# Decode attention: TensorE's steps taken in pairs

## The chip, the cores and the metric

The kernel runs on one core of one Trainium2 chip (trn2). The metric is the device time of one execution in microseconds (us). All inputs and outputs lie in the chip's memory (HBM).

## The reference, cut to what matters

One layer of a decoder: a mixer and an FFN, for a prompt of 256 tokens and for 8 samples of 8 new tokens each. The change touches the attention of the samples over their caches. Each sample b has 8 "fox" heads over 2048 cached keys (16 pages of 128, found by a page table, with a bias per key) and 12 "dilated" heads in three groups over cached windows of 128, 512 and 2048 keys.

```python
def fox_attend(q, k, v, bias_q, bias_k, q_pos, k_pos):
    s = jnp.einsum('bqhd,bshd->bhqs', q, k) * ATTN_SCALE + bias_q + bias_k      # cut
    p = jax.nn.softmax(jnp.where(causal, s, NEG_INF), axis=-1)
    return jnp.einsum('bhqs,bshd->bqhd', p, v)
def dilated_group_attend(q, k_all, v_all, q_idx, window, dil, table_g):
    kg, vg = k_all[:, idx_c], v_all[:, idx_c]                                    # every dil-th key
    s = jnp.einsum('bqhd,bqnhd->bhqn', q, kg) * ATTN_SCALE + rel
    lse = jax.nn.logsumexp(s, axis=-1)
    return jnp.einsum('bhqn,bqnhd->bqhd', jnp.exp(s - lse[..., None]), vg), lse
def merge_out(h, o_fox, o_dil, w_gate, b_gate, w_o_fox, w_o_dil, w_out):
    gates = jax.nn.sigmoid(jnp.einsum('bsd,de->bse', h, w_gate) + b_gate)
    g_fox, g_dil = jnp.split(gates, 2, axis=-1)
    return jnp.einsum('bse,ed->bsd', g_fox * y_fox + g_dil * y_dil, w_out)
```

The gates do not depend on the attention; the kernel computes most of them beside it.

## The kernel before

Everything is written out by hand, per engine, with semaphores; no scheduler moves anything. Each engine runs its own function `sequence(q, kb, vb)`. It is called as sequence 0 (keys of sample 0, no values), then seven times with the keys of sample kb = b and the values of sample vb = b-1, then once with the values of sample 7 alone. A sequence has 24 steps (STEPS), n = 0 to 23. Cached keys and values of a sample come in 23 blocks (KPG) each: 16 pages, one block of the first window, two of the second, four of the third. A block is 512 KB, the first window's 256 KB.

A step n of TensorE before the change:

- `transposes(kb, n)`: the keys of block n are turned, four 128x128 pieces into PSUM bank 2 (L1042) and four into bank 3 (L1047). ScalarE copies bank 2 to SBUF (L1428, semaphore ke_a), VectorE bank 3 (L1872, ke_b). Each bank has one buffer, so the next transposes wait for these copies.
- `gate_part(q, n)`: a share of the gate projection. A unit is 128 output channels, in 16 parts (128 input channels each) of three matmuls (L1031 to L1033, 320 columns). GATE_UNITS gives the units per sequence (2, 3, 3, 3, 4, 3, 3, 3, 1), spread evenly: with three units each step of a sequence has two parts, six matmuls.
- `fox_scores(kb, n // 2 - 1)` in even steps from 2 to 16: scores of two key blocks, eight matmuls into four column tiles of the array, 32 columns wide (L1067). VectorE adds the bias from PSUM to SBUF and takes the maximum (`fox_out`, L1877).
- `dil_scores` in steps 17 to 23 (L1081), column tiles too. `turn_fox` in steps 19 to 22: transposes of the fox probabilities (L1097), which ScalarE copies (`fox_probs`). The exponential that they need is ScalarE's `fox_exp`, in its steps 17 and 18, L1437.
- `values(vb, n)`: values of block n with the probabilities of sample vb, four matmuls for a page, in column tiles (L1127, L1133). `fox_new_values` (L1142) and `dil_new_values` (L1152) add the new tokens.
- `turn_dil` (L1104), `turn_out` (L1161), and `turn_dil_new` (L1111), which waits for ScalarE's copy of what `turn_dil` wrote.

The splits: gate weights come as fp32 panels and are split into a high part (ScalarE, L1395) and a low part (VectorE, L1837), in two halves per unit. The unit behind the next one is split 4 steps (for an even unit) or 1 step (for an odd one) after a unit is done, and its second half a step later (`splits_due`). In VectorE's program a step is: `keys_b(n)`, in even steps `fox_out`, then what `gates_after` has due. In ScalarE's it is `keys_a(n)`, then the softmax's part, then `gates_after`.

GpSimd issues the loads in the order key block n, value block n. kraw has 3 buffers, vraw 4: a load of block n waits until block n-3 is transposed, or block n-4 of the values is used. At step 1 it issues four bias loads for the sample (L705). SP issues the gate weights.

Of the kernel before, what the change touches and what calls it, by code (L numbers as in the profile page):

```python
# [40 lines left out]
NPG = PAST // PAGE  # L41
# [6 lines left out]
KPG = NPG + 1 + 2 + 4  # L48
# [95 lines left out]
def build(nc, I, O, scratch):  # L144
    with ExitStack() as ctx:
# [198 lines left out]
        STEPS = KPG + 1  # L344
# [462 lines left out]
        def _(pe):  # L807
# [13 lines left out]
            for n in range(12):  # L821
                t, q = divmod(n, 4)
# [202 lines left out]
            def gate_part(q, n):  # L1025
                for u, k in gate_work(q, n):
                    if k == 0:
                        pe.wait_ge(lo_done, u + 1)
                        pe.wait_ge(acc_free, u + 1)
                    acc = ps[:, u % 2, 0:T]  # L1030
                    pe.matmul(acc, w_hi[:, u % 2, k, :], act_hi[:, k, :], start=(k == 0), stop=False)  # L1031
                    pe.matmul(acc, w_hi[:, u % 2, k, :], act_lo[:, k, :], start=False, stop=False)  # L1032
                    mm = pe.matmul(acc, w_lo[:, u % 2, k, :], act_hi[:, k, :], start=False, stop=(k == KT - 1))  # L1033
                    if k == KT - 1:
                        mm.then_inc(unit_done, 1)

            def transposes(b, s):
                n = b * KPG + s
                pe.wait_ge(k_ld[n % KRING], loads_before(b, s, KRING))
                wait_pos(pe, ke_a, n)  # L1040
                for j in range(4):
                    mm = pe.transpose(ps[:, 2, P * j:P * j + P], kraw[:, n % KRING, P * j:P * j + P], ident[:])  # L1042
                mm.then_inc(tr_a, 1)
                if s != NPG:
                    wait_pos(pe, ke_b, narrow(b, s))
                    for j in range(4):
                        mm = pe.transpose(ps[:, 3, P * j:P * j + P], kraw[:, n % KRING, P * (4 + j):P * (5 + j)], ident[:])  # L1047
                    mm.then_inc(tr_b, 1)
# [22 lines left out]
            def dil_scores(b, s):  # L1071

                pe.wait_ge(ke_a, b * KPG + s + 1)
                if s != NPG:
                    pe.wait_ge(ke_b, narrow(b, s) + 1)
                else:
                    pe.wait_ge(qd_ok, b + 1)
                    wait_pos(pe, pd_ev, 2 * b)
                for r, g, c, n in residues(s):
                    for h in range(HG):  # L1080
                        mm = pe.matmul(ps[32 * h:32 * h + DT, 5, P * g:P * g + P], qd[:, 32 * n + DT * h:32 * n + DT * h + DT],  # L1081
                                       kT[:, s // 2 % 2, HG * r + h, P * (s % 2):P * (s % 2) + P], start=(n == 0), stop=False, **mmx)
                if s == KPG - 1:
                    for g in range(NG):
                        for h in range(HG):
                            mm = pe.matmul(ps[32 * h:32 * h + DT, 5, NG * P + DT * g:NG * P + DT * g + DT],
                                           sT[:, HF + HG * g + h, DT * b:DT * b + DT],
                                           sT[:, NQ + HF + HG * g + h, DT * b:DT * b + DT], start=False, stop=(g == NG - 1), **mmx)
                mm.then_inc(sc_done, 1)
# [17 lines left out]
            def turn_dil_new(b):  # L1107

                pe.wait_ge(pd_ev, 2 * b + 1)
                for g in range(NG):  # L1110
                    mm = pe.transpose(ps[0:DT, 5, P * g:P * g + P], ds_[:, NG * P + DT * g:NG * P + DT * g + DT], ident[:])  # L1111
                mm.then_inc(pd_tr, 1)
# [53 lines left out]

            def sequence(q, kb, vb):

                for n in range(STEPS):
                    if kb is not None and n < KPG:  # L1170
                        transposes(kb, n)
                    gate_part(q, n)
                    if vb is not None and n == 2:
                        turn_dil(vb)
                        if vb > 0:
                            turn_out(vb - 1)
                    if vb is not None and n == 3:
                        turn_dil_new(vb)
                    if kb is not None:
                        if n == 2:  # L1180
                            pe.wait_ge(zero_ps, 1)
                            fox_new_scores(kb)
                        if 2 <= n <= NPG and n % 2 == 0:
                            fox_scores(kb, n // 2 - 1)
                        if n > NPG:
                            dil_scores(kb, n - 1)
                        if 19 <= n < 23:
                            turn_fox(kb, n - 19)
                    if vb is not None and n < KPG:
                        values(vb, n)  # L1190
                        if n == NPG:
                            fox_new_values(vb)
                        if n == KPG - 1:
                            dil_new_values(vb)

            sequence(0, 0, None)
            for b in range(1, DB):
# [970 lines left out]
```

## Time and profile before

| | us |
|---|---|
| median of 3 runs | 2484.23 |
| lowest, highest | 2477.99, 2488.96 |
| the profiled execution | 2484.29 |
| its span, first to last instruction | 2482.7 |
| TensorE matmul busy | 2348.4 |
| VectorE busy | 1065.7 |
| ScalarE busy | 812.7 |
| decode attention, from the first key transposes to the last values | about 578 to 1280 |

In the profile PE is TensorE, PEld its weight loads, DVE VectorE, ACT ScalarE, POOL GpSimd, SP the engine that only issues transfers. Busy matmul times overlap, since matmuls are pipelined; how long something takes on TensorE is read from start to start. Each fp32 matmul is recorded as two, so eight score matmuls stand as x16. "[0.50 <-DVE kT L1872]" behind a row is idle time in front of it and who ended it.

### The profile page before, as it was taken

What the parts mean: (1) busy time and instruction counts of PE and PEld (TensorE: products, weight loads), DVE (VectorE), ACT (ScalarE), POOL (GpSimd) and SP (SyncE); (2) the same over time, 40 slices, a digit from 0 to 9 for tenths busy, and PEclk for the clock granted to TensorE, in tenths of its full rate; (3) what the DMA queues carried; (4) which work ended last, traced back from release to release, by engine and by line L of the source; (5) the groups of instructions that cost most, each with busy time, mean ns of one, the idle gap of its engine ahead of it and who ended that gap; (6) DMA issues with size and microseconds to landing.
All of it is one profiled execution on the core that took longest, in us unless ns stands there. A gap on an engine that the chain in (4) does not pass through costs nothing.

```text
span 2482.7 us, 45242 instructions
## 1 busy us (share of the span) xinstructions
PE 2348.4 (95%) x18252; PEld 2140.8 (86%) x18252; DVE 1065.7 (43%) x1433; ACT 812.7 (33%) x982; POOL 468.8 (19%) x877
## 2 busy tenths in 40 slices
PE   7999999997889999999989996999999999999997
PEld 6999999996666666666659995999999999999997
DVE  6443443433333333333326436444444444444445
ACT  3233333332333333333312334333333332333334
POOL 2110000101333333333311232111111111111221
PEclk8999999998999999999989997999999999999998
DMA  8554343545899999999976654676676766688883
GB/s 251 158 168 148 113 148 128 183 132 169 288 339 346 342 313 346 351 339 309 339 255 208 193 160 135 228 238 238 227 248 219 250 230 235 226 282 267 286 301 101
DMA packets 340126, 585.85 MB, mean 236 GB/s; under 512 B 20624, under 2 KB 283092, under 8 KB 336304
## 3 DMA queue, kind: packets, MB, share of 16 engines
q0 software_dynamic: 70752, 309.02, 35.2%
q1 hardware_dynamic: 269232, 274.86, 34.8%
q8 instruction: 99, 1.62, 0.3%
q14 instruction: 43, 0.34, 0.0%
HBM read 564.06 MB, written 109.39 MB: 271 GB/s over the span
## 4 chain that ended last, share of the span: by engine, by line
PE 79%; DMA 11%; issue 4%; DVE 3%; ACT 2%; POOL 1%; POOLq 0%; SPq 0%; DVEq 0%; ACTq 0%
PE ps L815 14%; PE ps L817 14%; PE ps L816 14%; DMA kraw<-in_cache_fox_k 6%; PE ps L853 6%; PE ps L855 6%; PE ps L854 6%; PE ps L1042 3%; PE ps L1047 2%; DMA kraw<-in_cache_win_k 2%; PE ps L1067 2%; PE ps L1127 1%; PE ps L1031 1%; PE ps L1033 1%; PE ps L1032 1%
## 5 line engine op out<-in xcount | busy, mean ns | idle before, releaser
L1626 DVE TENSOR_TENSOR w_lo<-raw,w_hi 128x2048 fp32r<-128x2048 f32 (+2 forms) x250 | 525.5, 2102 | 791.7 <-ACT w_hi L1295 785.4
L1295 ACT ACTIVATE w_hi<-raw 128x2048 fp32r<-128x2048 f32 (+2 forms) x250 | 439.2, 1757 | 1054.0 <-PE ps L817 741.5
L815 PE MATMUL ps<-act_hi,w_hi 128*128 128x320 f32 x1616 | 500.7, 310 | 5.7 <-DVE gs L2059 5.7
L817 PE MATMUL ps<-act_hi,w_lo 128*128 128x320 f32 x1616 | 500.5, 310 | 0.0
L816 PE MATMUL ps<-act_lo,w_hi 128*128 128x320 f32 x1616 | 500.5, 310 | 0.0
L853 PE MATMUL ps<-act_hi,w_hi 128*128 128x320 f32 x1040 | 327.6, 315 | 0.0
L855 PE MATMUL ps<-act_hi,w_lo 128*128 128x320 f32 x1040 | 321.4, 309 | 0.0
L854 PE MATMUL ps<-act_lo,w_hi 128*128 128x320 f32 x1040 | 321.3, 309 | 0.0
L815 PEld LDWEIGHTS ps<-act_hi,w_hi 128*128 128x128 f32 x1616 | 304.4, 188 | 5.9 <-issue 5.9
L816 PEld LDWEIGHTS ps<-act_lo,w_hi 128*128 128x128 f32 x1616 | 304.4, 188 | 0.0
L817 PEld LDWEIGHTS ps<-act_hi,w_lo 128*128 128x128 f32 x1616 | 304.3, 188 | 0.0
L1872 DVE COPY kT<-ps 128x512 f32<-128x512 f32 x176 | 121.4, 690 | 232.0 <-PE ps L1047 231.5
L1428 ACT ACTIVATE kT<-ps 128x512 f32<-128x512 f32 x184 | 109.7, 596 | 314.3 <-PE ps L1042 314.1
L853 PEld LDWEIGHTS ps<-act_hi,w_hi 128*128 128x128 f32 x1040 | 195.5, 188 | 0.8 <-issue 0.5
L854 PEld LDWEIGHTS ps<-act_lo,w_hi 128*128 128x128 f32 x1040 | 195.5, 188 | 0.1
L855 PEld LDWEIGHTS ps<-act_hi,w_lo 128*128 128x128 f32 x1040 | 195.2, 188 | 0.0
L1042 PEld LDWEIGHTS ps<-ident,kraw 128*128 128x128 f32 x736 | 80.6, 144 | 108.3 <-issue 49.9
L785 POOL TENSOR_TENSOR tick<-tick 1x1 f32<-1x1 f32 x144 | 28.5, 198 | 718.1 <-PE ps L817 708.0
L1042 PE MATMUL ps<-ident,kraw 128*128 128x128 f32 x736 | 124.3, 293 | 33.3 <-DMA kraw<-in_cache_fox_k 28.4
L1031 PE MATMUL ps<-act_hi,w_hi 128*128 128x320 f32 x400 | 145.0, 362 | 2.0 <-DVE w_lo L1626 2.0
L1033 PE MATMUL ps<-act_hi,w_lo 128*128 128x320 f32 x400 | 126.4, 316 | 0.0
L1032 PE MATMUL ps<-act_lo,w_hi 128*128 128x320 f32 x400 | 126.3, 316 | 0.0
(374 smaller groups left out, 3753.6 us busy)
## 6 DMA issues: line engine op xcount, KB each, us to landing
raw<-in_w_gate_up SPq DMA_DIRECT2D x88, 1024.0 KB, 6.3
kraw<-in_cache_fox_k POOLq DMA_DIRECT2D x128, 512.0 KB, 6.9
vraw<-in_cache_fox_v POOLq DMA_DIRECT2D x128, 512.0 KB, 7.5
raw<-in_w_in SPq DMA_DIRECT2D x60, 1024.0 KB, 7.6
raw<-in_w_gate SPq DMA_DIRECT2D x32, 1024.0 KB, 15.3
raw<-in_w_down SPq DMA_DIRECT2D x32, 1024.0 KB, 6.1
out_win_k_sample<-in_cache_win_k POOLq DMA_DIRECT2D x64, 510.0 KB, 5.8
out_win_v_sample<-in_cache_win_v POOLq DMA_DIRECT2D x64, 510.0 KB, 4.2
```

What stands on the lines that cost most here:

```text
L815: pe.matmul(ps[:, bk_, 0:T], w_hi[:, slot, k, :], xh[:, x_k, :], start=(k == k0), stop=False)
L816: pe.matmul(ps[:, bk_, 0:T], w_hi[:, slot, k, :], xl[:, x_k, :], start=False, stop=False)
L817: mm = pe.matmul(ps[:, bk_, 0:T], w_lo[:, slot, k, :], xh[:, x_k, :], start=False, stop=(k == k1 - 1))
L853: pe.matmul(acc, w_hi[:, u % 2, k, :], act_hi[:, k, :], start=(k == 0), stop=False)
L854: pe.matmul(acc, w_hi[:, u % 2, k, :], act_lo[:, k, :], start=False, stop=False)
L855: mm = pe.matmul(acc, w_lo[:, u % 2, k, :], act_hi[:, k, :], start=False, stop=(k == KT - 1))
L1031: pe.matmul(acc, w_hi[:, u % 2, k, :], act_hi[:, k, :], start=(k == 0), stop=False)
L1032: pe.matmul(acc, w_hi[:, u % 2, k, :], act_lo[:, k, :], start=False, stop=False)
L1033: mm = pe.matmul(acc, w_lo[:, u % 2, k, :], act_hi[:, k, :], start=False, stop=(k == KT - 1))
L1042: mm = pe.transpose(ps[:, 2, P * j:P * j + P], kraw[:, n % KRING, P * j:P * j + P], ident[:])
L1295: act.activation(w_hi[:, slot, 0:kt, :], raw[:, pslot, 0:kt, P * slot:P * slot + P], ACT.Copy).then_inc(hi_done, 1)
L1626: dve.tensor_tensor(w_lo[:, slot, 0:kt, :], raw[:, pslot, 0:kt, P * half:P * half + P], w_hi[:, slot, 0:kt, :].bitcast(F32), ALU.subtract) ...
```

## The change

Only TensorE's `sequence` changes. It takes two steps at a time. The gate matmuls of both stand between the two key transposes; behind the second come the fox scores, and both steps' dilated scores and values in one stretch. The transposes of the probabilities move beside the key transposes: parts 0 and 2 behind the transposes of steps 19 and 21, part 1 behind those of step 20, part 3 in front of the last stretch. `turn_dil_new` moves from step 3 to step 2. What TensorE computes, and the programs of the other engines, stay.

```diff
--- before.py
+++ after.py
@@ -1166,32 +1166,40 @@
 
             def sequence(q, kb, vb):
 
-                for n in range(STEPS):
-                    if kb is not None and n < KPG:
+                for n in range(0, STEPS, 2):
+                    if kb is not None:
                         transposes(kb, n)
+                        if n == 20:
+                            turn_fox(kb, 1)
                     gate_part(q, n)
+                    gate_part(q, n + 1)
                     if vb is not None and n == 2:
                         turn_dil(vb)
                         if vb > 0:
                             turn_out(vb - 1)
-                    if vb is not None and n == 3:
-                        turn_dil_new(vb)
                     if kb is not None:
+                        if n == 22:
+                            turn_fox(kb, 3)
+                        elif n + 1 < KPG:
+                            transposes(kb, n + 1)
+                        if n in (18, 20):
+                            turn_fox(kb, n - 18)
                         if n == 2:
                             pe.wait_ge(zero_ps, 1)
                             fox_new_scores(kb)
-                        if 2 <= n <= NPG and n % 2 == 0:
+                        if 2 <= n <= NPG:
                             fox_scores(kb, n // 2 - 1)
-                        if n > NPG:
-                            dil_scores(kb, n - 1)
-                        if 19 <= n < 23:
-                            turn_fox(kb, n - 19)
-                    if vb is not None and n < KPG:
-                        values(vb, n)
-                        if n == NPG:
-                            fox_new_values(vb)
-                        if n == KPG - 1:
-                            dil_new_values(vb)
+                    if vb is not None and n == 2:
+                        turn_dil_new(vb)
+                    for m in (n, n + 1):
+                        if kb is not None and m > NPG:
+                            dil_scores(kb, m - 1)
+                        if vb is not None and m < KPG:
+                            values(vb, m)
+                            if m == NPG:
+                                fox_new_values(vb)
+                            if m == KPG - 1:
+                                dil_new_values(vb)
 
             sequence(0, 0, None)
             for b in range(1, DB):
```

TensorE in a pair of fox steps of sequence 1, before (gates, fox scores, values, key transposes, gates):

```order
L1031 MATMUL ps<-act_hi,w_hi 128x320
L1032 MATMUL ps<-act_lo,w_hi 128x320
L1033 MATMUL ps<-act_hi,w_lo 128x320
L1067 MATMUL ps<-kT,qf 16x256 x8
L1127 MATMUL ps<-vraw,pt 16x256 x4
L1042 MATMUL ps<-ident,kraw 128x128 x4
L1047 MATMUL ps<-ident,kraw 128x128 x4
L1031 MATMUL ps<-act_hi,w_hi 128x320
```

and after (gates, key transposes, fox scores, values of both blocks, next transposes, gates):

```order
L1031 MATMUL ps<-act_hi,w_hi 128x320
L1032 MATMUL ps<-act_lo,w_hi 128x320
L1033 MATMUL ps<-act_hi,w_lo 128x320
L1042 MATMUL ps<-ident,kraw 128x128 x4
L1047 MATMUL ps<-ident,kraw 128x128 x4
L1067 MATMUL ps<-kT,qf 16x256 x8
L1127 MATMUL ps<-vraw,pt 16x256 x8
L1042 MATMUL ps<-ident,kraw 128x128 x4
L1047 MATMUL ps<-ident,kraw 128x128 x4
L1031 MATMUL ps<-act_hi,w_hi 128x320
```

The second key transposes now stand in front of the scores, and the next key transposes follow right behind the values.

TensorE at the probabilities' transposes (L1097), before, behind the gates of a step:

```order
L1033 MATMUL ps<-act_hi,w_lo 128x320
L1081 MATMUL ps<-kT,qd 8x128 x8
L1097 MATMUL ps<-ident,fs 128x128 x4
L1133 MATMUL ps<-vraw,pg 16x256 x4
L1042 MATMUL ps<-ident,kraw 128x128 x4
L1047 MATMUL ps<-ident,kraw 128x128 x4
L1031 MATMUL ps<-act_hi,w_hi 128x320
L1032 MATMUL ps<-act_lo,w_hi 128x320
```

and after, the same part and its neighbours:

```order
L1042 MATMUL ps<-ident,kraw 128x128 x4
L1047 MATMUL ps<-ident,kraw 128x128 x4
L1097 MATMUL ps<-ident,fs 128x128 x4
L1081 MATMUL ps<-kT,qd 8x128 x8
L1133 MATMUL ps<-vraw,pg 16x256 x4
L1081 MATMUL ps<-kT,qd 8x128 x8
L1133 MATMUL ps<-vraw,pg 16x256 x4
```

Between tiles before, now directly behind the key transposes.

VectorE, step 12 and 13 of sequence 1; its line numbers are 8 higher after the change, its order is the same (key copy of step 12, bias add, low part of the weight split, key copies of steps 13 and 14):

```order
L1880 COPY kT<-ps 128x4x128
L1885 ISA fs,fm<-ps,fb 128x256
L1885 ISA fm 128x1
L1845 TENSOR_TENSOR w_lo<-raw,w_hi 128x1024
L1880 COPY kT<-ps 128x4x128 x2
```

The copy of step 13 stands behind the bias add and the split, though the transposes that it copies are now issued before the scores that the bias add waits for.

## Rows read from the trace of the kernel before

**Rows 1.** Waits of TensorE from 700 to 1250 us: us in total, times, longest us.

```profile
PE ps L1042 <- DMA kraw<-in_cache_fox_k: 17.0, 20, 1.9
PE ps L1127 <- DMA vraw<-in_cache_fox_v: 16.8, 8, 4.5
...
PE ps L1047 <- DVE kT L1872: 1.5, 3, 0.5
```

**Rows 2.** Busy time by stretch: stretch, its length, each engine's busy us, PEclk, DMA share, GB/s.

```profile
578.00:660.00 82.00, 62.66 (x615) 49.35 (x613) 33.45 (x70) 29.99 (x46) 22.41 (x39) 0.86 0.73 212
660.00:1235.00 575.00, 529.96 (x5784) 382.75 (x5781) 195.85 (x427) 198.44 (x346) 188.92 (x354) 0.97 0.96 339
1235.00:1290.00 55.00, 44.48 (x338) 25.05 (x332) 12.67 (x22) 13.34 (x23) 14.01 (x25) 0.84 0.81 268
```

**Rows 3.** TensorE in order of time, one pair of steps: start us, us, what, count.

```profile
1009.25 1.06 PE L1067 MATMUL ps<-kT,qf 128*16 128x256 f32 x16
1010.12 0.61 PE L1127 MATMUL ps<-vraw,pt 128*16 128x256 f32 x8
1010.66 0.66 PE L1042 MATMUL ps<-ident,kraw 128*128 128x128 f32 x4
1011.16 0.60 PE L1047 MATMUL ps<-ident,kraw 128*128 128x128 f32 x4
1011.51 0.39 PE L1031 MATMUL ps<-act_hi,w_hi 128*128 128x320 f32 x1
...
1012.32 0.31 PE L1033 MATMUL ps<-act_hi,w_lo 128*128 128x320 f32 x1
1012.56 0.62 PE L1127 MATMUL ps<-vraw,pt 128*16 128x256 f32 x8
1013.12 0.66 PE L1042 MATMUL ps<-ident,kraw 128*128 128x128 f32 x4
```

**Rows 4.** TensorE in order of time in sequence 0: gate matmuls, then key transposes.

```profile
608.81 0.31 PE L1033 MATMUL ps<-act_hi,w_lo 128*128 128x320 f32 x1
608.96 0.60 PE L1042 MATMUL ps<-ident,kraw 128*128 128x128 f32 x4
609.40 0.60 PE L1047 MATMUL ps<-ident,kraw 128*128 128x128 f32 x4
```

**Rows 5.** TensorE in order of time, two steps with dilated scores.

```profile
714.79 0.62 PE L1081 MATMUL ps<-kT,qd 128*8 128x128 f32 x16
715.23 0.62 PE L1133 MATMUL ps<-vraw,pg 128*16 128x256 f32 x8
...
716.93 0.66 PE L1047 MATMUL ps<-ident,kraw 128*128 128x128 f32 x4 [0.50 <-DVE kT L1872]
...
718.40 0.62 PE L1081 MATMUL ps<-kT,qd 128*8 128x128 f32 x16
718.95 0.66 PE L1097 MATMUL ps<-ident,fs 128*128 128x128 f32 x4
719.54 0.63 PE L1133 MATMUL ps<-vraw,pg 128*16 128x256 f32 x8
```

**Rows 6.** VectorE in order of time: bias add, weight split, key copy; and the copy at 716.

```profile
716.20 0.68 DVE L1872 COPY kT<-ps 128x512 f32<-128x512 f32 x1
...
1010.37 0.42 DVE L1877 CUSTOM_DVE_ANT_0 fs<-ps,fb 128x256 f32<-128x256 f32 x1 [0.42 <-PE ps L1067]
...
1010.72 1.22 DVE L1837 TENSOR_TENSOR w_lo<-raw,w_hi 128x1024 fp32r<-128x1024 f32 x1
1011.86 0.68 DVE L1872 COPY kT<-ps 128x512 f32<-128x512 f32 x1
```

**Rows 7.** ScalarE in order of time: table load and first exponential of the softmax.

```profile
1048.74 1.28 ACT L1437 ACT_TABLE_LOAD   x1
1050.03 1.15 ACT L1437 ACTIVATE fs<-fs,fm 128x1024 f32<-128x1024 f32 x1
```

**Rows 8.** DMA issues by line: count, KB each, median us to landing.

```profile
kraw<-in_cache_fox_k POOLq DMA_DIRECT2D x128, 512.0 KB, 6.9
```

## The prediction

> **What bounds the kernel now.** I read four views: the waits of TensorE, the busy time by stretch, the order of time on TensorE over a few steps, and the order of time on the engines that empty PSUM for it. The change touches only the stretch of decode attention: 184 key blocks (23 for each of 8 samples b), one step each, and a 24th step per sample that has gates alone. The stretch has three parts [rows 2]. In the first (keys of sample 0, no values; sequence 0) TensorE is busy 62.66 of 82 us. In the long middle (seven sequences with keys of b and values of b-1) it is busy 529.96 of 575 us. In the tail (values only) it is busy 44.48 of 55 us, with the loads as its pace. In the middle the DMA engines are busy 0.96 of the time too, so two resources are nearly full together. TensorE waited for key blocks 20 times, 17.0 us, and for value blocks 8 times, 16.8 us with a longest of 4.5 us [rows 1]. Those long ones stand at the head of each sequence, where the bias rows are loaded. The rest of the middle runs at TensorE's pace, so an instruction gap on TensorE is time of the kernel there, as long as nothing takes its place.
>
> One pair of steps before, by starts [rows 3] (T = eight key transposes, G = six gate matmuls, S = fox scores, V = values of one block): S to V 0.87 us, V to T 0.54 to 0.56, inside T 0.50, then 0.35 to the first G, G to V 1.05. The pair T G V T G S V is 0.85 + 1.05 + 0.56 + 0.85 + 1.05 + 0.87 + 0.54 = 5.77 us.
>
> **The change part by part.** The pair becomes T G G T S V V.
> - Pitch inside G: 0.145 us (last gate to the transposes behind it, 0.15 [rows 4], so going from gates to transposes costs nothing). The first gate behind transposes has 0.23 us: 1012.32 minus 1011.51 is 0.81, less four pitches. Two G in one are 0.23 + 11 x 0.145 = 1.83 us.
> - Transposes behind gates: 0.44 for the first four [rows 4] instead of 0.50. The four before tiles take 0.59 between tile matmuls on both sides (L1097) [rows 5], less 0.06 for the entry: 0.53. The second T is 0.97 us.
> - V before another V, without the way back to the full array: eight S matmuls take 0.87, so four take 0.43 instead of 0.55.
> - Sum: 0.85 + 1.83 + 0.97 + 0.87 + 0.43 + 0.55 = 5.50 us, 0.27 to 0.28 less. With 12 pairs in 7 sequences: 84 x 0.28 = 23.5 us.
> - The four transposes of the probabilities (L1097) per sample stood between tile matmuls: dilated scores to V is 0.44 directly and 0.55 + 0.59 with them [rows 5], 0.70 more. Beside other transposes they cost 0.44. That is 0.26 less, 28 times in the middle, 7.3 us, and 1.0 us in sequence 0.
> - In sequence 0 there are no values. Two steps had T G T G S; T G G T S has the same sum, since the saved entries are paid back at the transposes in front of the tiles. Nothing there but the 1.0 us.
> - In the tail the loads set the pace (268 GB/s, TensorE idle 10 of 55 us [rows 2]). I take 0; at most 12 x 0.2 us.
> - The small transposes L1111 go from step 3 to step 2, behind S. What they wait for (ScalarE's copy of the first four) has the second T and S, 1.8 us, as its cover. I take 0; 0.5 us a sequence if the cover fails.
>
> Gain on TensorE alone: 31.8 us.
>
> What it adds is on VectorE, whose own order stays. It copies the second half of the keys of step n, adds the bias to S (L1877), does a weight split if one is due in step n, and then copies the keys of step n+1. Before, the transposes of n+1 came after S, so this queue had a whole step. Now they stand before S, and the next transposes into the same bank come after S V V. Counted from the start of S, those want the bank at 0.87 + 0.43 + 0.55 + 0.50 = 2.35 us. VectorE starts the bias add 1.12 us after S (1009.25 to 1010.37) [rows 3, 6], its next instruction 0.35 later, and a copy takes 0.69. TensorE goes on 0.05 us after a copy ends (716.20 + 0.68 against 716.93 [rows 5, 6]). Free at 2.21 us: a pair without a split just passes, with 0.14 us to spare.
> - With a split behind the bias add (next start 1.14 us later [rows 6]) the bank is free at 3.34 us: TensorE waits 1.0 us, and all behind it. By the rule that sets the splits one falls on an even step from 4 to 12 in 11 cases of the middle (12; 4, 8; 12; 4, 6; 4, 8; 12; 4, 8 in sequences 1 to 7): 11 us.
> - On step 16 there are four (sequences 1, 3, 4, 6), with more tile work in front: 0.6 us each, 2.4 us.
> - The softmax. ScalarE begins it when the maximum is there, behind S of step 16, which now stands after the transposes of 17. Table 1.28 and exponential 1.15 us [rows 7], then where one is due a weight split, and only then the next keys. I get 0.4 us more than now in three sequences and 1.2 in sequence 4: 2.4 us.
> - Sequence 0 has no V as cover. The bank is wanted at 0.87 + 0.12 + 0.50 = 1.49 us and free at 2.21: 0.7 us in each of 7 pairs, 1.8 in that of step 16, 6.8 us. About 2 us of small key waits in that stretch vanish in them: 4.7 us.
>
> Cost: 11 + 2.4 + 2.4 + 4.7 = 20.5 us. Bounds of this block: 0 (if something of these waits is always there already) and 41, twice, if later key loads follow each late bank.
>
> The loads. GpSimd asks for key block n when block n-3 has been transposed. Before, the lead was three steps less a T, 3 x 2.89 - 0.85 = 7.8 us. Now it is 7.35 us for both blocks of a pair (3.65 us into a pair to the start of the next but one, 11.0). A block lands in 6.9 us [rows 8]. With the DMA engines at 0.96 nothing is gained where they are full: at the head of each sequence and while a panel of gate weights comes in, some 3 to 4 of 12 pairs. I take 5 us given back; bounds 0 and all of the net gain, 11.
>
> Sum: -31.8 + 20.5 + 5 = -6 us. The profiled execution took 2484.29 us, at the median of 2484.23: 2478 us.
>
> **The rivals.**
> - The gain comes whole: the bank waits fall where TensorE would wait for blocks anyhow, or VectorE gets to the copy sooner. For it: the splits come near panel loads, where waits for keys stand now. Against it: the loads keep 0.96. Without the bank waits -31.8, less some 7 us more of block waits, as 0.96 cannot go much over 1 (0.04 x 575 = 23 us is all that is left in the middle): -25, 2459 us.
> - The loads are the bound: what TensorE saves, it waits for blocks, and of the bank waits sequence 0's remain. For it: rows 2. Against it: between the heads the pair has run at 5.77 us. 0 to +3 us, 2485 us.
> - Slower: emptying PSUM decides in every pair, the place being the transposes behind S V V. The spare there is 0.14 us. If VectorE comes that much later, or V V is shorter, all 41 pairs without a split wait as well; with 0.5 us each, the size of the wait seen now for this bank [rows 5], it is 20 us more: 2498 us. It decides from 0.14 us on. For it: the spare is a difference of pipelined starts. Against it: each start was read at full clock. The Trainium skill, "TensorEngine Tiling (Array Packing)", section "PSUM Bottleneck", says that with tiles TensorE speeds up but the emptying of PSUM does not and may become the limit; by that rule this case is the outcome, and the trace so far shows the bank's copy as the releaser of L1047 three times, 1.5 us in all [rows 1].
> - That the change does nothing: two mode changes a pair go, and I have read their price from starts, so this has almost no chance.
>
> **How the numbers follow.** Likeliest case (2478, own range 2468 to 2487) 0.50; gain whole 0.22; loads the bound 0.15; slower by every pair 0.13. Less than 0.5%, 12.4 us, cannot be told from no change. The first case passes that bound downward about one time in seven, the second nearly always, the fourth about two times in three upward. Faster 0.28, same 0.62, slower 0.10. For 8 in 10 the range reaches from the second case to just short of the fourth: 2458 to 2494 us.
>
> **What would show it.** The pair from T to T without a split 5.50 us, with one 6.5. TensorE's waits before L1047 released by VectorE's key copy, 1.5 us before [rows 1], near 15 to 20 us in all, the longest 1.0 us, and seven of 0.7 in sequence 0. The probability transposes 0.44 us behind T. Waits for kraw and vraw in sum a few us above 34. I am wrong if the L1047 waits stay under 5 us, if they appear in pairs without a split in the middle, or if the waits for blocks grow by over 15 us.

## The result: no faster, and slower by 7 us

| | median of 20 runs, us | lowest, highest |
|---|---|---|
| before | 2480.49 | 2473.82, 2493.98 |
| after | 2487.47 | 2477.86, 2499.22 |

The ratio is 1.0028, with a 95% interval of 1.0015 to 1.0041: 7 us more (3.7 to 10.2). That is inside the range and inside 0.5%, but the sign of the forecast, 6 us less, was wrong. The profiled execution of after took 2493.41 us (span 2491.8), at the upper end of its runs; a second one, r1_after, took about 2480. Of before there is a second one too, r0_before (span 2479.8). Single profiles of one kernel differ by up to 13 us, so below I use both where a sum over a stretch is taken.

What TensorE waited for in the profile after, 700 to 1250 us, in the columns of [rows 1]:

```profile
PE ps L1127 <- DMA vraw<-in_cache_fox_v: 24.8, 6, 6.0
PE ps L1042 <- DMA kraw<-in_cache_fox_k: 19.6, 22, 2.6
PE ps L1047 <- DVE kT L1880: 9.9, 15, 0.8
...
PE ps L1111 <- ACT pn L1461: 2.4, 1, 2.4
```

The wait for VectorE's copy of the key bank rose from 1.5 us in 3 places [rows 1] to 9.9 us in 15 (in the second profiles from 2.5 us in 5 to 9.9 in 15). The wait for value blocks rose from 16.8 to 24.8 us, and its longest from 4.5 to 6.0. The second profile of either kernel says the same, r0_before first, then r1_after:

```profile
PE ps L1127 <- DMA vraw<-in_cache_fox_v: 18.0, 7, 4.6
PE ps L1042 <- DMA kraw<-in_cache_fox_k: 13.2, 18, 1.5
```

```profile
PE ps L1127 <- DMA vraw<-in_cache_fox_v: 29.6, 8, 6.6
PE ps L1042 <- DMA kraw<-in_cache_fox_k: 16.9, 18, 2.7
```

The same three stretches as in [rows 2], after:

```profile
578.00:660.00 82.00, 62.16 (x607) 49.95 (x605) 30.00 (x65) 29.13 (x46) 21.80 (x38) 0.88 0.69 195
660.00:1235.00 575.00, 509.68 (x5725) 394.55 (x5729) 193.93 (x432) 200.62 (x347) 188.25 (x354) 0.96 0.97 340
1235.00:1290.00 55.00, 40.35 (x341) 20.58 (x330) 10.09 (x19) 10.90 (x20) 11.65 (x22) 0.74 0.72 237
```

In the middle TensorE is busy 20 us less of 575 than in [rows 2], for 1% fewer records (5725 against 5784); in the second profiles it is 15 us less for 30 records more. The DMA share is 0.97 where it was 0.96, and 340 GB/s where it was 339. So TensorE got its work done in less time, and most of that time turned into waits.

A pair of steps on TensorE in the profile after, then a pair with a split in it, in the columns of [rows 3]:

```profile
767.47 0.66 PE L1042 MATMUL ps<-ident,kraw 128*128 128x128 f32 x4
...
770.17 0.60 PE L1042 MATMUL ps<-ident,kraw 128*128 128x128 f32 x4
770.60 0.60 PE L1047 MATMUL ps<-ident,kraw 128*128 128x128 f32 x4
771.13 1.06 PE L1067 MATMUL ps<-kT,qf 128*16 128x256 f32 x16
772.00 1.05 PE L1127 MATMUL ps<-vraw,pt 128*16 128x256 f32 x16
772.98 0.66 PE L1042 MATMUL ps<-ident,kraw 128*128 128x128 f32 x4
774.48 0.65 PE L1047 MATMUL ps<-ident,kraw 128*128 128x128 f32 x4 [0.84 <-DVE kT L1880]
...
779.55 0.66 PE L1042 MATMUL ps<-ident,kraw 128*128 128x128 f32 x4
```

From transposes to transposes the first takes 772.98 - 767.47 = 5.51 us (forecast 5.50), the second 779.55 - 772.98 = 6.57 (forecast 6.5). VectorE in the second, in order of time:

```profile
772.25 0.42 DVE L1885 CUSTOM_DVE_ANT_0 fs<-ps,fb 128x256 f32<-128x256 f32 x1 [2.96 <-PE ps L1067]
...
772.61 1.22 DVE L1845 TENSOR_TENSOR w_lo<-raw,w_hi 128x1024 fp32r<-128x1024 f32 x1
773.74 0.68 DVE L1880 COPY kT<-ps 128x512 f32<-128x512 f32 x1
```

The bank had been full since 771.2, and VectorE stood idle 2.96 us in front of the bias add, since its order puts the scores first. Then came the split, and only then the copy, which ends at 774.42. TensorE goes on at 774.48: 1.50 us from the first four transposes to the second, where it is 0.50 without the wait, so the price is the 1.0 us of the forecast (the view counts 0.84 of it as idle). In order of time the 15 waits are eleven of 0.84 and four of 0.16; the four stand at step 16. These are the 11 and 4 splits that the forecast counted.

The transposes of the probabilities, after, behind those of the keys:

```profile
723.46 0.60 PE L1047 MATMUL ps<-ident,kraw 128*128 128x128 f32 x4
723.90 0.60 PE L1097 MATMUL ps<-ident,fs 128*128 128x128 f32 x4
724.25 0.39 PE L1031 MATMUL ps<-act_hi,w_hi 128*128 128x320 f32 x1
```

They start 0.44 us behind those of the keys, and the gates follow 0.35 us later.

Waits of TensorE in sequence 0 (578 to 660 us), after:

```profile
PE ps L1042 <- DMA kraw<-in_cache_fox_k: 8.6, 2, 8.4
PE ps L1047 <- DVE kT L1880: 6.4, 7, 3.3
```

Of the 6.4 us, 3.3 is one wait that before has as well (3.3 us, once, in the same view of before). The other six are the new ones, 0.5 us each as idle time. In order of time, a pair of sequence 0:

```profile
610.24 1.06 PE L1067 MATMUL ps<-kT,qf 128*16 128x256 f32 x16
611.23 0.66 PE L1042 MATMUL ps<-ident,kraw 128*128 128x128 f32 x4
612.46 0.66 PE L1047 MATMUL ps<-ident,kraw 128*128 128x128 f32 x4 [0.57 <-DVE kT L1880]
```

From start to start it is 1.23 us instead of 0.50: 0.73, the forecast's 0.7.

Sequence 0 has one more cost, which is not in the forecast. In before, the first fox scores run at 592.58, and then TensorE waits for the load of step 3 until 600.94. In pairs these scores stand behind the transposes of step 3, so they come after that wait and no longer in front of it:

```profile
600.46 1.12 PE L1042 MATMUL ps<-ident,kraw 128*128 128x128 f32 x4 [8.41 <-DMA kraw<-in_cache_fox_k]
603.10 1.91 PE L1067 MATMUL ps<-kT,qf 128*16 128x256 f32 x16 [0.42 <-DVE fm L1885]
604.94 1.12 PE L1042 MATMUL ps<-ident,kraw 128*128 128x128 f32 x4
```

From the transposes of step 3 to those of step 4 it is 604.94 - 600.46 = 4.48 us, the same in r1_after, against 2.57 and 2.56 in the two traces of before: 1.9 us. From step 4 to step 16, where five of the six new bank waits lie, it is 30.4 and 29.2 against 27.7 and 27.5.

To see where the time goes I read the start of single instructions in each trace and divided the stretch in three: sequence 0 from the first key transpose to the first `turn_dil`; six sequences from there to the seventh `turn_dil`; the last from there to the last `dil_new_values`.

| us | sequence 0 | six of the middle | last |
|---|---|---|---|
| before, r0_before | 85.0, 82.2 | 500.6, 503.8 | 112.9, 114.0 |
| after, r1_after | 89.1, 89.0 | 502.0, 495.1 | 113.7, 111.9 |
| mean difference | +5.4 | -3.7 | -0.6 |

The middle of one kernel differs by 7 us between its two profiles. Two kernels below, e2 and e3, have the middle of after unchanged: 498.1 and 498.6 us, so -3.7 holds.

These sum to +1; the two profiled pairs differ by +4 in their spans, and the 20 runs by +7. So 3 us of the profiled difference lie outside the attention of the samples, where the program is the same, and some 3 us more are in the runs but not in these profiles. I could not place those.

### The profile page after: what moved, and what is told of

Same layout as the page of the kernel before. It is cut to its first block, busy times and chain, and to the rows that moved or that the text cites. A ratio compares the mean times of both kernels' runs of the same rounds, so it can differ in the third digit from the quotient of the medians.

```text
span 2491.8 us, 45242 instructions
## 1 busy us (share of the span) xinstructions
PE 2333.2 (94%) x18252; PEld 2159.0 (87%) x18252; DVE 1060.5 (43%) x1433; ACT 813.7 (33%) x982; POOL 468.2 (19%) x877
## 4 chain that ended last, share of the span: by engine, by line
PE 79%; DMA 10%; DVE 4%; issue 4%; POOL 1%; ACT 1%; POOLq 0%; SPq 0%; DVEq 0%; ACTq 0%
PE ps L815 14%; PE ps L816 14%; PE ps L817 14%; DMA kraw<-in_cache_fox_k 6%; PE ps L853 6%; PE ps L855 6%; PE ps L854 6%; PE ps L1047 3%; PE ps L1042 2%; PE ps L1067 2%; PE ps L1031 2%; PE ps L1032 1%; PE ps L1033 1%; PE ps L1127 1%; DMA raw<-in_w_gate 1%
## 5 line engine op out<-in xcount | busy, mean ns | idle before, releaser
L785 POOL TENSOR_TENSOR tick<-tick 1x1 f32<-1x1 f32 x144 | 29.2, 203 | 716.4 <-PE ps L817 706.2
```

## The experiments

Each kernel was timed against before in the same batch; the ratios are to before.

**Both kernels again.** No edit.

> The kernel before once more, for a second profile. In the first one TensorE waited 37.6 us for key and value blocks in the middle and stood at the slow clock level for 34 us of it; five profiles of kernels with the paired middle show 44 to 49 us and 41 to 48 us. If pairs are the cause, this one lies under those again (35 to 40 us and 30 to 38 us). If the first profile was chance, it lies among them.

> The changed kernel once more, as the mark for the three beside it. Both theories expect what was seen, a ratio to before of 1.0015 to 1.0041. The trace shows how far one profile stands for the next: waits of TensorE for VectorE's key copy near 6 us in sequence 0 and 10 us in the middle; the waits for value blocks at the heads of the sequences, and those of the tail, may differ by some us from the first profile.

Measured: 2480.29 us, 0.9994 [0.9982, 1.0006], and 2486.4 us, 1.0027 [1.0014, 1.0040]. The difference stands.

**The copy ahead of the bias add.** After, with VectorE's copy of odd steps 3 to 17 in front of the scores' bias add:

```diff
-                        if n < KPG and n != NPG:
+                        if n < KPG and n != NPG and not (n % 2 and 2 < n <= NPG + 1):
                             keys_b(kb, n)
+                        if n % 2 == 0 and 2 <= n <= NPG:
+                            keys_b(kb, n + 1)
```

> VectorE takes the key copy of each odd step from 3 to 17 in front of the bias add of the even step before it. Theory 1 (the waits for the bank cost the change its gain): the waits before L1047 in sequence 0 and the middle fall from 16 us to under 3, and the time falls by 12 to 16 us against the changed kernel, to about 10 us under the kernel before. Theory 2 (the loads take back what TensorE saves): the same waits fall, sequence 0 gets its 4 to 5 us back, but in the middle the waits for key and value blocks grow by as much as the bank waits fall, and the time falls by 4 to 6 us, to that of the kernel before.

Measured: 2478.03 us, 0.9995 [0.9984, 1.0007], 8.4 us less than after (give or take 4), between what the two theories expected. TensorE's waits of this kernel, 700 to 1250 us:

```profile
PE ps L1127 <- DMA vraw<-in_cache_fox_v: 29.8, 9, 7.1
PE ps L1042 <- DMA kraw<-in_cache_fox_k: 20.0, 24, 2.9
PE ps L1067 <- DVE fm L1885: 4.4, 6, 0.7
```

The 9.9 us of bank waits are gone (0.6 is left, once), for 1.9 us more in front of the scores (4.4 against 2.5). VectorE now copies before it adds, and the bank is free when the next transposes come:

```profile
771.04 0.69 DVE L1880 COPY kT<-ps 128x512 f32<-128x512 f32 x1 [1.93 <-PE ps L1047]
772.06 0.42 DVE L1885 CUSTOM_DVE_ANT_0 fs<-ps,fb 128x256 f32<-128x256 f32 x1 [0.33 <-PE ps L1067]
```

So the bank waits cost time, though they stand beside waits for blocks: with light loads (l_e1, below) the same edit brings 9.6 us, about as much. Without them the paired kernel only equals before; most of the 31.8 us saved on TensorE is still not there. In sequence 0 the edit shortens the stretch from step 4 to step 16 to 27.3 us, as short as before. The 1.9 us in front of it stay (from step 3 to step 4 it is 4.76), and the whole sequence takes 88.9 us in this one profile, as long as in after, since it waits some 1 us longer each for a load at its start (9.55 against 8.41) and for the value block at its end (4.7 against 3.5).

**One end of the stretch step by step.** TensorE's old loop for the last sequence alone, and for sequence 0 alone:

```diff
-            sequence(DB, None, DB - 1)
+            single_sequence(DB, None, DB - 1)
```

```diff
-            sequence(0, 0, None)
+            single_sequence(0, 0, None)
```

> Only the last sequence (values of sample 7 alone) is taken step by step as before. If pairs cost the tail its 4 us by bunching the releases of the value buffers, the stretch from the last key scores to the last values falls by 3 to 4 us and so does the time. If the 4 us were chance of one profile, stretch and time stay within 1 us.

Measured: 2484.38 us, 1.0013 [1.0000, 1.0025]: 2 us less than after, which these runs can't tell from nothing.

> Only sequence 0 (keys of sample 0 alone) is taken step by step as before. Theory 1 and the prediction's own term: sequence 0 is 4 to 5 us shorter than in the changed kernel (from the first to the second bias load 61 to 62 us instead of 66) and the time falls by as much. Rival: the loads behind set when the middle starts, and the time stays within 1 us.

Measured: 2479.65 us, 1.0008 [0.9994, 1.0022]: 7 us less than after. Its sequence 0 takes 85.9 us, against 89.1 and 89.0, and from step 3 to step 4 it is 2.57 us again. By time and by trace pairing costs 3 to 7 us in sequence 0.

**Lighter loads.** These leave work out, as their expectations say. For samples 1 to 7 `l` halves the value loads and drops the bias loads; in `x` key and value blocks bring a quarter, and the bias loads are dropped too. The edit of `l`, without VectorE's wait for the dropped loads:

```diff
-                pool.dma_start(vraw[:, n % VRING, 0:src.shape[1]], src)
+                w = src.shape[1] if n < KPG else src.shape[1] // 2
+                pool.dma_start(vraw[:, n % VRING, 0:w], src[:, 0:w])
...
-                        if n == 1:
+                        if n == 1 and kb == 0:
                             load_bias(kb)
```

> The order of before with the loads relieved: value blocks of samples 1 to 7 bring half of their columns (the rest is what stood in the buffer), and the bias rows of sample 0 serve all samples. It is the mark for the next one. Both theories: DMA share in the middle near 0.75, no long waits for value blocks, 25 to 45 us faster than before.

> The changed order with the same relief (half of the value columns, bias of sample 0 alone). Theory 2 (the loads take back what TensorE saves): with room in the loads the gain on TensorE shows, and this is 8 to 14 us faster than the relieved kernel of before (31.8 less 20.5 of my sum). Theory 1, that the bank waits or something else on the chip's engines cost as much as is gained: it is within 3 us of it or slower.

> The relieved loads (half of the value columns of samples 1 to 7, bias of sample 0 alone) with the changed order and the key copy of the odd step in front of the bias add. Theory 2 expects that here, where the loads have room, the bank waits are worth their length: 8 to 13 us faster than the relieved changed kernel, 2410 to 2415 us. Theory 1 expects the same here and the same 8 to 13 us at full loads, where 8.4 us were measured with both sequence 0 and the middle mended.

> The order of before with the loads taken far below their limit: key and value blocks of samples 1 to 7 bring a quarter of their columns, and the bias rows of sample 0 serve all (the rest of each block is what stood in the buffer). A mark for the next two: DMA share in the middle near 0.4, waits for blocks in the middle under 3 us, a pair of steps at 5.77 us.

> The changed order with the same quarter loads. If my sum for TensorE and VectorE was right (31.8 us gained, 20.5 paid), 9 to 13 us faster than its mark. If the gain was sized too high, 5 to 8 us as with half of the values left out.

> The same quarter loads with pairs in the middle alone and the key copy of the odd step in front of the bias add. If the sum was right, 25 to 30 us faster than its mark (30.8 gained, 2.4 paid for the softmax). If the gain was sized too high, 15 to 20 us.

Measured (c1 is paired in the middle alone, with the copy first; see below):

| loads | before | after | with the copy first |
|---|---|---|---|
| full | 2480.5 | 2487.5 | e1 2478.0, c1 2474.3 |
| l | 2430.7, 0.9802 [0.9774, 0.983] | 2423.2, 0.9766 [0.974, 0.9792] | l_e1 2413.5, 0.9719 [0.9697, 0.974] |
| x | 2416.9, 0.9753 [0.9729, 0.9776] | 2413.1, 0.9729 [0.9708, 0.9749] | x_c1 2397.7, 0.9656 [0.9634, 0.9679] |

l_before was to be 25 to 45 us under before, at a DMA share of 0.75; it is 49, at 0.86. The same edit of TensorE's order gives +7 with full loads and -7.5 with `l` (8 to 14 were expected). With `x` it gives -3.8, under both expectations (9 to 13 and 5 to 8), and x_c1 is 19.2 us faster than x_before, in the lower one (15 to 20) and not in the one that goes with my sum (25 to 30). The traces say where the rest of the sum went. In `x` the middle no longer waits for blocks. Busy time of x_before and then x_after, 660 to 1150 us, columns of [rows 2]:

```profile
660.00:1150.00 490.00, 480.47 (x5365) 347.69 (x5366) 185.93 (x408) 184.82 (x324) 168.29 (x313) 1.00 0.47 149
```

```profile
660.00:1150.00 490.00, 471.48 (x5501) 369.67 (x5505) 185.53 (x422) 190.97 (x332) 173.50 (x322) 1.00 0.48 153
```

and the largest waits of x_after from 660 to 1165 us (line numbers are 2 higher; L1049 is L1047):

```profile
PE ps L1049 <- DVE kT L1882: 11.9, 18, 0.8
PE ps L1044 <- ACT kT L1438: 3.2, 5, 1.2
...
PE ps L1044 <- DMA kraw<-in_cache_fox_k: 0.8, 1, 0.8
```

Here pairing saves what TensorE's sum says. The six middle sequences go from 455.6 to 441.6 us, 14.0 less; by my terms without the loads they would be (23.5 + 7.3 - 11 - 2.4 - 2.4) x 6/7 = 12.9 less. With the copy first they take 433.8, 21.8 less, where all but the softmax's 2.4 us would give 24.3. The ends lose: sequence 0 2.4 us (80.7 to 83.1), the last one 4.5 (98.8 to 103.3), so by the traces 7.1 are left, by the times 3.8. The last one loses in its tail: from the last but one `dil_new_values` to the last takes 40.6 us against 34.8 (x_c1, with the old order there, 33.1). The values of two steps now stand together, so their buffers come free together and the next loads are asked for together; that is my reading of it, and no run tests it. TensorE waits there for values, in x_after, 1150 to 1240 us:

```profile
PE ps L1129 <- DMA vraw<-in_cache_fox_v: 7.1, 4, 3.6
```

In x_before it is 2.7 us. With full loads the tail's pace is another, and it shows no such loss: 45.3 and 47.2 us before, 48.2 and 45.2 after.

**The bias loads.** At step 1 of each sequence GpSimd issues four loads (L705), which read 8 rows, each 8 times over. GpSimd and TensorE there, before:

```profile
726.07 2.27 POOL L705 DMA_DIRECT2D fb<-scratch_fb  x4
```

```profile
742.27 0.62 PE L1127 MATMUL ps<-vraw,pt 128*16 128x256 f32 x8 [4.08 <-DMA vraw<-in_cache_fox_v]
```

and after:

```profile
728.42 2.26 POOL L705 DMA_DIRECT2D fb<-scratch_fb  x4
```

```profile
744.80 1.05 PE L1127 MATMUL ps<-vraw,pt 128*16 128x256 f32 x8 [5.31 <-DMA vraw<-in_cache_fox_v]
```

From the issue of the bias loads to TensorE's use of the value block behind them it is 16.20 us before and 16.38 after. Over seven sequences, by the same reading, TensorE came to that block 11.8 us behind the issue in both traces of before, and waited 2.9 and 2.7 us. In the two of after it came 11.1 and 10.9 us behind, and waited 4.05 and 4.0. In one of the seven the block had landed before TensorE came, in both traces of before; over the other six, from issue to block, it is 15.1 and 14.9 us before, 15.6 and 15.4 after. So TensorE comes 0.8 us earlier and the block does not, rather later; why later is not shown.

Why TensorE comes earlier is in the order. The bias loads are issued when block 21's keys have been transposed. In pairs these transposes stand behind both gate parts, so 0.9 us of gate work moved from behind the issue to in front of it. But the dilated scores and values of step 20, 0.9 us too, moved the other way, from in front of these transposes to behind them. The two cancel. What is left is the gain itself: in a full sequence TensorE had seven separate stretches of column-tile work from the issue up to that block, and now has three.

From that block to the next issue it took 68.4 and 68.6 us, now 67.9 and 67.15: 1.0 less, where the light loads show 2.3 less for a whole sequence. So at this one place 0.8 us a sequence is saved and waited away, and with the later block the wait is 1.3 us longer, 9 us over seven sequences. Two pairs of kernels bear on it. In `f` the bias loads of samples 1 to 7 are left out (and VectorE's wait for them):

```diff
-                        if n == 1:
+                        if n == 1 and kb == 0:
                             load_bias(kb)
```

> The order of before with full value loads, but the bias rows of sample 0 serve all samples (seven of eight groups of four bias loads left out). If these loads make the long wait at the head of each sequence, the waits for value blocks in step 1 (some 20 us in the middle) go, and it is 25 to 40 us faster than before.

> The changed order with the bias loads of samples 1 to 7 left out. If what is given back goes at the heads of the sequences (behind the bias loads), this is 5 to 10 us faster than the same kernel in the order of before. If it goes all along the middle, because the key and value loads have no room, the two are within 3 us.

> The kernel before with the bias loads of samples 1 to 7 left out, once more and with more rounds: 2441 to 2445 us, six sequences of the middle in 470 to 475 us.

> The changed kernel with the same loads left out, with more rounds. If the heads take the gain back: the middle keeps its 9 to 11 us over six sequences, sequence 0 costs 4, and it is 3 to 8 us faster than the same kernel in the order of before. If the key and value loads take it all along: within 2 us, and the middle shorter by less than 5 us.

Measured: f_before 2442.13, 0.9843 [0.9818, 0.9868], and again 2443.27, 0.9851 [0.9829, 0.9873]; f_after 2442.96, 0.9856 [0.9826, 0.9886], and again 2441.85, 0.9853 [0.9829, 0.9877]. The means of nine runs each are 2443.5 and 2443.6, give or take 3. Without bias loads pairing costs nothing where it cost 7 us with them, so the heads account for about 7 us by the times, near the 9 that I read there. It gains nothing either, though. The profiles of `f` show the middle 8 us shorter (472.6 and 466.7 to 463.0 and 460.3; with all loads it was 3.7) and sequence 0 3.5 longer, which would be 4.5 less; the times don't show it. So neither expectation of f2_after came whole: the times fit the second, the middle the first. Who holds the rest shows beside `l`: it differs from `f` in one thing, that half of each value block is loaded, and there pairing gains 7.5 us and makes the middle 9.8 us shorter. In `x`, with a quarter of each key and value block, the middle is 14.0 us shorter. So the loads of the blocks themselves hold the rest.

In `p` the bias is written 8 times to memory ahead, so that 64 different rows are read. Nothing is left out:

```diff
-        fbd = nc.dram_tensor("scratch_fb", (DB, HF, NPG * P), F32, kind="Internal").ap()
+        fbd = nc.dram_tensor("scratch_fb", (DB, HF, DT, NPG * P), F32, kind="Internal").ap()
...
-                    rows = fbd[b, 2 * j:2 * j + 2].unsqueeze(1).broadcast_to([2, DT, PAST])
-                    pool.dma_start(fb[32 * j:32 * j + 2 * DT, :], rows)
+                    pool.dma_start(fb[32 * j:32 * j + 2 * DT, :], fbd[b, 2 * j:2 * j + 2].rearrange("h q n -> (h q) n"))
```

> The kernel before with the bias written eight times to memory ahead of the decode stretch (64 stores of 64 KB instead of 8), so that the four loads of each sample read 64 different rows instead of the same 8 rows eight times. If it is the repeated reading of the same rows that slows all packets (4 KB packets took 159 ns as a rule and about 400 ns beside these loads), the waits at the heads go and it is 20 to 35 us faster than before. If it is the writing of 64 rows of 8 KB each into one partition, nothing changes, and it is the same or slower by the stores.

Measured: 2466.2 us, 0.9943 [0.9923, 0.9962], 14 less. I had looked for 20 to 35. From issue to block it is 13.65 us there, with a wait of 1.5 (over the six heads with a wait). How the bias is read is a part of what these loads cost, not all. That it is the reading of the same rows is not shown: the edit also turns each load's source from 2 rows repeated 8 times into 16 rows in one dimension, and reading a row again does not make a packet slow by itself: the 8 KB packets from 660 to 1235 us, nearly all of them of these loads, have a median of 652 ns in before and 920 in p_before.

**The best of both.** Pairs in the seven middle sequences, the old loop at both ends, the copy first in the middle; then the same with the bias of `p`:

```diff
-            sequence(0, 0, None)
+            single_sequence(0, 0, None)
...
-            sequence(DB, None, DB - 1)
+            single_sequence(DB, None, DB - 1)
...
-                        if n < KPG and n != NPG:
+                        if n < KPG and n != NPG and not (q and n % 2 and 2 < n <= NPG + 1):
                             keys_b(kb, n)
+                        if q and n % 2 == 0 and 2 <= n <= NPG:
+                            keys_b(kb, n + 1)
```

> Pairs in the seven middle sequences alone, sequence 0 and the last one step by step as before, and in the middle the key copy of the odd step in front of the bias add. It leaves out all of my sum's costs but the softmax (2.4 us), and keeps 30.8 us of gain on TensorE. Theory 1 (bank waits and sequence 0 are what made the change slower): 15 to 25 us faster than before. Theory 2 (the loads have no room): 0 to 6 us faster than before, with bank waits under 2 us in the middle and 45 to 55 us of waits for blocks.

> All data loaded: pairs in the middle alone, key copy of the odd step in front of the bias add, and the bias written eight times so that no row is read twice. If the two add up it is 21 to 25 us faster than before (7.7 and 14.2 us, and some of the waits for blocks less): 2455 to 2461 us. If the loads stay the bound all along the middle, the bias stores bring their 14 us and the pairs 3 us at most: 2463 to 2467 us.

Measured: c1_best 2474.32 us, 0.9969 [0.9958, 0.998], 6 to 8 less than before, just above what the second theory expected (0 to 6) and far from the first (15 to 25). p_c1 2463.35 us, 0.993 [0.9911, 0.9948], the fastest with all the work in it, as its second expectation had it; beside p_before the pairs bring 3 us, less than the runs can tell. Both are faster than before and after, by less than 1%. In c1 TensorE still waits this much from 700 to 1250 us:

```profile
PE ps L1127 <- DMA vraw<-in_cache_fox_v: 30.1, 9, 6.6
PE ps L1042 <- DMA kraw<-in_cache_fox_k: 17.2, 25, 1.6
```

47 us for blocks, where [rows 1] has 34 and r0_before 31. Of some 25 us that these pairs save over seven sequences where no block is waited for (x_c1, 21.8 in six), 13 to 16 stand here as waits.

The granted clock moved too. From 660 to 1235 us, p_before and then p_c1:

```profile
660.00:1235.00 575.00, 533.07 (x5877) 379.87 (x5875) 202.64 (x438) 205.81 (x360) 192.12 (x366) 0.99 0.98 348
```

```profile
660.00:1235.00 575.00, 523.59 (x5876) 402.61 (x5876) 203.42 (x439) 208.35 (x361) 192.07 (x364) 0.96 0.98 348
```

These means stand for 12 and 46 us at the lower level (1.2 GHz). For before and after they are 0.97 and 0.96, 32 and 44 us; for r0_before and r1_after 34 and 44. The stretches at the lower level follow waits, in after mostly those at the heads, as at the value block that is waited for until 744.80:

```profile
736.20:739.60 3.40, 3.29 (x29) 2.60 (x28) 2.11 (x7) 3.35 (x7) 1.06 (x2) 1.00 1.12 176
739.60:743.00 3.40, 0.00 (x0) 0.00 (x0) 0.35 (x4) 0.44 (x1) 1.05 (x2) 0.87 1.04 164
743.00:746.40 3.40, 1.11 (x9) 0.20 (x9) 0.00 (x0) 0.00 (x0) 0.00 (x0) 0.50 1.03 406
746.40:749.80 3.40, 3.40 (x17) 3.40 (x18) 0.69 (x1) 0.60 (x1) 0.53 (x1) 0.62 1.03 419
```

The clock falls while TensorE is idle, and it works on at half the rate for some microseconds more. How much it worked there can be read from slices of 0.5 us between 660 and 1235 us: at the lower level TensorE is busy for 27.5 and 27.9 us in the two traces of before, 34.3 and 35.5 in those of after, 11.0 in p_before and 41.4 in p_c1. About half of that is lost by my estimate, so 3.5 us more in after than in before, and 15 us more in p_c1 than in p_before. These are upper estimates, since slower work can also fall where the next block would be waited for.

In `p` this is the larger part. There the six middle sequences take 484.6 us before and 484.8 in p_c1, though the same pairs save 21.8 where no block is waited for. From 700 to 1235 us the waits for key and value pages grow by 6 us only, from 30.3 to 36.4; with the 15 us of the clock that makes 21. No run holds the clock where it was, so this rests on the traces alone.

## Why the prediction was wrong, step by step

- **The pair**, 5.50 us: right, 5.51. So is the split pair, 6.57 for 6.5, with 1.0 us of it for the bank.
- **The transposes of the probabilities**, 0.44: right. With the pairs and the costs in the middle it makes 12.9 in six sequences, and 14.0 was measured where no block is waited for (`x`).
- **The bank waits**, 15 to 20 us in all: 9.9 + 6.4 = 16.3 us in 22 places, 3.3 of it an old one, so the number holds only with it. Eleven splits at 1.0 us each: right. The four of step 16: 0.16 us of idle each, under the 0.6 of the forecast, 1 to 2 us less in all. In sequence 0 0.7 each: right. The kernels with the copy first show that they are paid (8.4 us with full loads, 9.6 with light ones), against the rival by which they would fall beside block waits; 8.4 is less than the 12 to 16 that my sum gives for them, and the copy first has a cost of its own (1.9 us in front of the scores).
- **Sequence 0**, 4.7 us: 5.4 by the traces, about 7 by e3's time. The size is right, in part by luck: 1.9 us of it are the first fox scores behind the load of step 3, which the sum does not have. Six new bank waits came where it has eight with 6.8 us, and the one of step 16 is 0.7 and 1.2 us from start to start, not 1.8.
- **Every pair waits** (the slower rival, 2498): false. All 15 waits of the middle fall on splits; a pair without one passes with 5.51 us, in spite of a spare of only 0.14 us.
- **The tail**, 0: not told from 0 with full loads (e2: 2 us), but a loss of 5.8 us with the lightest ones (34.8 to 40.6), of a kind that I had not thought of; that two value buffers coming free at once make it is my reading.
- **The loads**: this is the step that failed. "I take 5 us given back; bounds 0 and all of the net gain, 11." My terms for the middle without it are -15.0 us in seven sequences, the light loads show -14.0 x 7/6 = -16, and with full loads the traces show -3.7 x 7/6 = -4: 11 to 12 us were given back in the middle alone, at the bound and not at 5. Up to 3.5 of them are the lower clock behind the waits, a term that the sum has not at all. The waits for blocks say the same: 33.8 and 31.2 us before, 44.4 and 46.5 after, 13 more, where I had "a few us". I had asked how much lead each load has in a steady pair. What decided was a place outside any pair: the head of a sequence, where a window of 15 us is set by the bias loads, from their issue to the block behind them. The waits there grew by 9 us, and with the bias loads (`f`) about 7 us of loss go by the times, 4 by the traces of the middle. I had [rows 1] with its longest wait of 4.5 us there, and did not follow which TensorE instruction lets the bias loads go, nor how much of my gain lies between it and that block, where nothing can be gained.

Put together, -15 in the middle, +12 given back, +5 in sequence 0 is +2 by the traces; with 5 instead of 12 it is -5, the forecast. The loads are 7 of the 13 us between forecast and result, sequence 0 one more. The other 5 or so are not placed: 3 of them lie outside the attention in the profiles.

The nearest of my rivals is "the loads are the bound" (2485 us, given 0.15): its number holds, its mechanism holds in part. Were it the whole of it, taking the bank waits of the middle away would have brought nothing. e1 brought 8.4 us, and by its trace the middle is 3 us shorter than the mean of the four traces with the middle of after, so the times speak more clearly here than the traces.

## What to carry to other kernels

Where an engine and the DMA queues are both near 0.96, price an edit of the engine's order at the places where loads are let go: which instruction frees the load, how long the block behind it takes regardless, and how much of the gain lies between the two. That part is waited away, and the wait can lower the clock for the work behind it. When transposes are pulled ahead of other work, the queue of the engine that empties their bank has to be reordered with them; here that alone was worth 8 us, more than the change itself. And use a new order only in the sequences that have its cover: the same pairs cost time in sequence 0, and paid in the middle. Work that ran ahead of a long wait for a load must not be moved behind it, as the first scores of sequence 0 were.

## What the runs showed of the hardware

Four loads of 128 KB per sample, 28 for samples 1 to 7, cost the kernel 37 us (f_before) though they are 3.7 MB of 586. The 37 us also hold what GpSimd spends on issuing them, 2.3 us a sample (at 726.07), and its wait for VectorE's maxima in front; no run separates these. Each load writes 16 rows of 8 KB, made of 2 different ones; with 16 different rows 14 of the 37 us go, by the reading or by the shape of the source. A kernel that loads small tables by repeating a row should look at what lies beside such a load.
